# Prompt attention and three quarters of the output projection in one block of a hybrid decoder step

## The chip, the cores and the metric

The kernel runs on one core of a Trainium2 chip. A core has five engines with a queue of instructions each: PE (TensorE, the matrix engine), DVE (VectorE), ACT (ScalarE), POOL (GpSimd), and SP, which here only starts DMAs. Each engine runs its own queue strictly in the order written; engines wait for one another only at semaphores. The metric is the device time of one execution in microseconds (us), the median of several runs.

## The reference

One layer of a decoder, for a prompt (512 tokens and 16 learned "meta" tokens ahead of them) and 8 sample sequences of 4 tokens. All numbers are fp32. What matters here, for the prompt rows:

```python
# A: sparse attention. Per block of 128 queries: indexer scores over 16 small heads, top-128 keys, then 4 heads of attention
s = relu(einsum('bthd,bsd->bths', qi, ki)); sc = einsum('bths,bth->bts', s, wi)      # 16 heads, masked to the past
_, idx = lax.top_k(sc, topk)                                                          # topk = 128
logits = q . k[idx] + rel_bias[t5_bucket(dist)]; out = softmax(logits) @ v[idx]       # 4 heads x 128
# B (Mamba-2) and C (gated DeltaNet) give the other 1536 of 2048 columns, from the same normed input
mix = concatenate([o_a, o_b, o_c])          # 512 + 768 + 768 columns
x = x + mix @ w_out                         # 2048 x 2048
hm = rmsnorm(x, g_mlp); x = x + square(relu(hm @ w_up)) @ w_down    # 2048 x 8192 x 2048
```

Only the first 512 of the 2048 rows of `w_out` meet attention's output `o_a`; the other 1536 meet `o_b` and `o_c`, which are ready before attention starts.

## The kernel before

The program is a row of blocks with a barrier of all engines between them: an input projection (with sample attention beside it), convolutions and gates, the scans of B and C, `gate_and_norm`, `attention_inputs`, `attend_prompt`, and `output_and_mlp`.

**Projections.** An fp32 weight tile is split into a high and a low part, each good for the fast matmul form (fp32r), and three products are added: high by high, high weight by low activation, low weight by high activation. For the output projection a chunk is 128 output columns by 2048 rows (1 MB). SP loads it in two halves to `om_raw`; DVE masks it (`TENSOR_SCALAR`, `om_mask`), makes the high part (`CAST`), POOL subtracts for the low part (`TENSOR_TENSOR` to `om_ring`), and PE does 16 k tiles x 3 products x 2 halves of the 544 tokens = 96 matmuls into two PSUM banks. DVE then adds the banks to `om_x`. There are `NOUT` = 16 chunks, and the ring has two slots. The activations are split in the same way once, 16 tiles, at the start (L2846, L2850 on DVE, L2692 on POOL). After all 16 chunks, the second norm follows: squares (ACT) are summed by PE with a matrix of ones (L2740), DVE multiplies each of 16 tiles of x by the gain and splits it (L2870, L2846, L2850), and takes the reciprocal of the root (L2876); meanwhile the first MLP chunk runs as its tiles come. The MLP itself is a loop of 8 groups of 16 chunks, untouched by the change.

**Attention.** `attention_inputs` loads q, k, v and indexer rows, normalises q and k (DVE), turns them by PE transposes, and builds the relative bias (8 matmuls of a one-hot table, copied by DVE, written to DRAM and read back skewed into `toe`). `attend_prompt` goes over 5 query tiles, four of 128 rows and one of 16, with 128, 256, 384, 512 and 528 keys. For tile i >= 1: `choose(i)` adds up 16 indexer heads (PE score, ACT relu, DVE multiply and add, L1973), then 16 rounds of `MAX8` (L1979) and `MATCH_REPLACE8` (L1980) mark the 128 best keys; `soften(i)` does for each of 4 heads: PE scores, DVE adds mask and bias (L1994) and takes the maximum (L1996), ACT exponential, DVE reciprocal and scaling (L1998, L1999), PE transpose, ACT copy, PE product with v. One tile is finished before the next is begun on DVE. Score banks and the other buffers are double.

## Time and profile before

| what | value |
|---|---|
| median of 3 runs | 3852.7 us (3848.6 to 3852.73) |
| the profiled execution, its own time | 3852.63 us |
| its span in the profile | 3850.8 us |
| PE / DVE / POOL / ACT busy | 85% / 58% / 37% / 14% |
| `gate_and_norm` | 1650 to 1719 us |
| `attention_inputs` | 1719 to 1766.5 us |
| `attend_prompt` | 1766.5 to 2007.4 us |
| output projection with its start | 2007.4 to 2243.3 us |
| second norm beside the first MLP chunk | 2243.3 to 2277.2 us |
| the other 127 MLP chunks and the output | 2277.2 to 3850.8 us |

The first stage in the rows of stages below, 312 to 564 us, is the input projection beside the samples' selection.

Rows of the trace name the engine, the line of the kernel, the operation, the tile written and the tiles read. PEclk is the share of the full 2.4 GHz that TensorE was granted. Busy time of an engine that waits for another is no measure of the stage; what ends the waits is.

### The profile page before, as it was taken

Reading aid. Unit: us, or ns where it says so; the run is one execution under the profiler, and the core shown is the slowest. Engines: PE = TensorE matmul, PEld = TensorE weight load, DVE = VectorE, ACT = ScalarE, POOL = GpSimd, SP = SyncE. Lnnn points to the kernel's source line nnn. Section 1 sums busy time; section 2 is a strip of 40 time slices with the busy share of each in tenths; the row PEclk is TensorE's granted clock in tenths of the full one; section 3 lists DMA queues with packets and bytes.
Section 4 is the critical chain, followed back from the end, with each engine's and each line's share of the span. In section 5 each row is a group of like instructions: output and inputs, shape, how many; then the busy total and the mean of one; then the engine's idle time right before and its main releaser. Section 6 shows DMA issues by size and latency. Waiting matters only on the chain. (4 is left out here: it accounts for less than half of the span.)

```text
span 3850.8 us, 54189 instructions
## 1 busy us (share of the span) xinstructions
PE 3272.8 (85%) x22335; PEld 2978.1 (77%) x22335; DVE 2220.1 (58%) x3256; ACT 526.7 (14%) x1009; POOL 1409.3 (37%) x839
## 2 busy tenths in 40 slices
PE   7979997998944877715449989999999999999998
PEld 6927887997633777313129979999999999999998
DVE  6038985993176654446765465455555554646564
ACT  4132121121143111121121010000000000000000
POOL 4363332583332223110014344344444343444442
PEclk9999998999966987755669989999999999999999
DMA  5333332685420002142014213322323232223232
GB/s 175 88 94 100 90 89 82 188 273 155 142 86 24 1 1 66 28 159 85 0 60 140 81 55 90 86 88 85 92 82 91 80 88 89 88 86 91 78 93 96
DMA packets 412524, 352.99 MB, mean 92 GB/s; under 512 B 24106, under 2 KB 369290, under 8 KB 410901
## 3 DMA queue, kind: packets, MB, share of 16 engines
q1 hardware_dynamic: 383376, 285.58, 25.3%
q0 software_dynamic: 13440, 42.02, 3.4%
q10 hardware_dynamic: 15472, 21.90, 1.6%
q8 instruction: 190, 3.11, 0.3%
q14 instruction: 46, 0.38, 0.0%
HBM read 308.06 MB, written 42.61 MB: 91 GB/s over the span
## 5 line engine op out<-in xcount | busy, mean ns | idle before, releaser
L2686 POOL TENSOR_TENSOR om_ring<-om_raw,om_mask 128x1024 fp32r<-128x1024 f32 x288 | 741.0, 2573 | 1032.2 <-DVE om_ring L2789 1032.2
L2726 PE MATMUL om_ps<-om_h,om_ring 128*128 128x272 f32 x7680 | 986.8, 291 | 62.8 <-POOL om_h L2692 35.1
L2726 PEld LDWEIGHTS om_ps<-om_h,om_ring 128*128 128x128 f32 x7680 | 977.5, 191 | 70.1 <-issue 60.8
L2726 PE MATMUL om_ps<-om_hid,om_ring 128*128 128x272 f32 x6144 | 770.8, 288 | 0.0
L2726 PEld LDWEIGHTS om_ps<-om_hid,om_ring 128*128 128x128 f32 x6144 | 770.0, 188 | 0.0
L2789 DVE CAST om_ring<-om_mask 128x1024 fp32r<-128x1024 f32 x288 | 483.3, 1678 | 10.0
L320 POOL TENSOR_TENSOR w_ring<-w_raw,w_mask 128x1024 fp32r<-128x1024 f32 (+2 forms) x110 | 259.5, 2379 | 369.1 <-DVE w_mask L451 211.5
L371 PE MATMUL pm_ps<-h,w_ring 128*128 128x280 f32 x2688 | 364.2, 297 | 26.1 <-issue 11.5
L371 PEld LDWEIGHTS pm_ps<-h,w_ring 128*128 128x128 f32 x2688 | 355.5, 192 | 35.1 <-issue 28.0
L2797 DVE TENSOR_TENSOR om_x<-om_x,om_ps 128x272 f32<-128x272 f32 x288 | 112.8, 433 | 459.3 <-PE om_ps L2726 458.8
L389 PE MATMUL pq_ps<-w_ring,h 128*128 128x512 f32 (+2 forms) x1440 | 291.6, 365 | 7.6 <-POOL w_ring L320 7.5
L389 PEld LDWEIGHTS pq_ps<-w_ring,h 128*128 128x128 f32 x1440 | 249.0, 189 | 50.1 <-issue 8.3
L2914 ACT ACTIVATE om_relu<-om_relu 128x272 f32<-128x272 f32 x128 | 49.9, 432 | 1416.5 <-DVE om_relu L2818 1416.5
L2818 DVE SCALAR_TENSOR_TENSOR om_relu<-om_ps,om_rstd 128x272 f32<-128x272 f32 x128 | 50.4, 436 | 319.3 <-PE om_ps L2726 319.3
L2786 DVE TENSOR_SCALAR om_mask<-om_raw 128x1024 uint32<-128x1024 uint32 x288 | 209.2, 726 | 20.1 <-DMA om_raw<-in_w_out 17.6
L404 ACT ACTIVATE w_ring<-w_mask 128x1024 fp32r<-128x1024 f32 (+2 forms) x128 | 123.5, 1008 | 414.3 <-DVE w_mask L451 314.4
L451 DVE TENSOR_SCALAR w_mask<-w_raw 128x1024 uint32<-128x1024 uint32 (+2 forms) x128 | 85.7, 694 | 147.4 <-DMA w_raw<-in_w_in 146.5
L1950 POOL TENSOR_TENSOR ap_bm<-toe,ap_sc 128x128 f32<-128x128 f32 (+4 forms) x20 | 18.5, 945 | 295.3 <-DVE ap_sc L1982 194.6
L2406 POOL DMA_INDIRECT as_rows<-in_cache_v,as_offs x64 | 62.8, 982 | 106.1 <-PE as_o_bank L2571 93.5
L1881 PE MATMUL ap_t<-ident,ap_lg 128*128 128x128 f32 (+2 forms) x60 | 13.1, 334 | 102.3 <-DVE ap_lg L1999 102.3
L371 PEld LDWEIGHTS pi_ps<-h,w_ring 128*128 128x128 f32 x768 | 98.9, 188 | 0.1
L371 PE MATMUL pi_ps<-h,w_ring 128*128 128x280 f32 x768 | 98.9, 291 | 0.0
(475 smaller groups left out, 3438.0 us busy)
## 6 DMA issues: line engine op xcount, KB each, us to landing
om_raw<-in_w_up SPq DMA_DIRECT2D x128, 512.0 KB, 4.1
om_raw<-in_w_down SPq DMA_DIRECT2D x128, 512.0 KB, 3.6
w_raw<-in_w_in SPq DMA_DIRECT2D x112, 512.0 KB, 4.1
om_raw<-in_w_out SPq DMA_DIRECT2D x32, 512.0 KB, 4.1
as_qb<-q_rows SPq DMA_DIRECT2D x32, 256.0 KB, 5.1
projT<-pm_stage ACTq DMA_DIRECT2D x56, 140.0 KB, 2.1
conv_x<-projT SPq DMA_DIRECT2D x28, 280.0 KB, 2.8
xT_scratch<-ln_xT SPq DMA_DIRECT2D x1, 4480.0 KB, 16.0
```

The costliest lines, as they stand in the source:

```text
L320: eng.tensor_tensor(f32r(ring[:, n % 2, 1, half_of(q, n)]), raw[:, q, whole(q, n)], mask[:, q, whole(q, n)], ALU.subtract).then_inc(split[ ...
L371: ins = pe.matmul(ps[(b + y) % banks][:, 0:HALF], piece(a, k), f32r(h[:, x, k, two_halves(y)]), start=first, stop=last)
L389: ins = pe.matmul(ps[(b + m) % banks][:, 0:w], f32r(h[:, x, ld.k0 + k, tok]), piece(a, k), start=first, stop=last)
L404: act.activation(f32r(ring[:, n % 2, 0, half_of(q, n)]), mask[:, q, whole(q, n)], ACT.Copy).then_inc(hi_ready[q], 1)
L451: dve.tensor_scalar(bits(mask[:, q, whole(q, n)]), bits(raw[:, q, whole(q, n)]), HIGH, None, ALU.bitwise_and).then_inc(masked[q], 1)
L2406: pool.indirect_dma_start(self.rows[:, n % RING, :], None, table, bass.IndirectOffsetOnAxis(ap=self.offs[:, x, j:j + 1], axis=0)).then_inc ...
L2686: pool.tensor_tensor(f32r(ring[:, s, 1, half_of(q)]), raw[:, q, :], mask[:, q, :], ALU.subtract).then_inc(split[q], 1)
L2726: ins = pe.matmul(ps[bank][:, 0:HM], w, f32r(src[:, b, k, kept_half(half)]), start=first, stop=last)
L2786: dve.tensor_scalar(bits(mask[:, q, :]), bits(raw[:, q, :]), HIGH, None, ALU.bitwise_and).then_inc(masked_w[q], 1)
L2789: dve.tensor_copy(f32r(ring[:, s, 0, half_of(q)]), mask[:, q, :]).then_inc(hi_ready[q], 1)
L2797: dve.tensor_tensor(dst, dst, ps[b][:, 0:HM], ALU.add).then_inc(evac[b], 1)
L2818: dve.scalar_tensor_tensor(out=relu[:, 2 * (c % 2) + half, :], in0=ps[b][:, 0:HM], scalar=0.0, in1=rstd[:, kept_half(half)], op0=ALU.max, ...
```

## The change

1. `attention_inputs`, `attend_prompt` and 12 of the 16 k tiles of the output projection become one block, `attend_and_project`. The 12 k tiles are those of B and C. The projection there goes over 16 units of 128 output columns (72 matmuls and 768 KB of weights each, split in halves of 128x768), and adds to x tiles that are read from DRAM and written back (`ao_xin`). High parts of these weights are made by ACT, low parts by POOL; DVE masks and adds.
2. The order on every engine comes from `in_time`, which merges generators by due times written out by hand (`AS_FROM`, `AS_PER`, `UNIT` and others); the times only set the order.
3. Within attention DVE interleaves three query tiles: a round of selection on tile i, one head sum of tile i+1, and softmax steps of tile i-1. The last tile's 16 indexer heads are packed: 8 heads x 16 queries fill the 128 rows of one matmul, so that two relu tiles and a small matmul with `ao_selw` replace 16 steps.
4. The relative bias is built in `gate_and_norm` (PE, then ACT copies), ahead of its own work.
5. `output_and_mlp` keeps 4 k tiles: 4 chunks of 512 columns, 16 steps `t` of 24 matmuls, and gain and splitting of 12 of the 16 x tiles for the MLP are done inside that loop.

The core of the diff:

```diff
 def gate_and_norm(nc, dram, consts, sb):
         @block.scalar
         def _(act):
+            for x in range(8):
+                act.wait_ge(row, x + 1)
+                act.activation(rows_of_bias[:, x // 2, 384 * (x % 2):384 * (x % 2 + 1)], row_ps[x % 2][:, :], ACT.Copy
+                               ).then_inc(row_out, 1)
             for i in range(5):
...
+AS_FROM, AS_PER = (34.0, 46.0, 72.5, 111.0, 144.5, 178.0), (0.75, 1.65, 2.4, 2.1, 2.1, 3.0)
+FIRST_UNIT, UNIT = 10.0, 11.4
...
+def in_time(*streams):
+    due = [next(stream, None) for stream in streams]
+    while any(at is not None for at in due):
+        who = min((at, n) for n, at in enumerate(due) if at is not None)[1]
+        due[who] = next(streams[who], None)
...
+def attend_and_project(nc, dram, consts, sb):
...
+        def _(pe):
+            def weights():
+                for n in range(UNITS):
+                    for k in range(KB):
+                        yield unit_at(n) + UNIT / KB * k
+                        if k % (KB // PARTS) == 0:
+                            pe.wait_ge(hi_ready[k // (KB // PARTS)], n + 1)
+                            pe.wait_ge(split[k // (KB // PARTS)], n + 1)
...
+            in_time(inputs(), scores(), turns_of_weights(), values(), weights())
...
+        def _(dve):
...
+                for i in range(1, 5):
+                    for r in range(TOPP // 8):
+                        yield when(i, r)
+                        step(dve.max(best[0:n, r % 2, :], x))
+                        step(dve.match_replace(x, best[0:n, r % 2, :], x, TAKEN))
+                        if i < 3:
+                            add_head(i + 1, r)
...
+                        if i >= 2 and r % 4 == 1:
+                            yield logits_at(i - 1, r // 4)
+                            logits(i - 1, r // 4)
+                        if i >= 2 and r % 4 == 3:
+                            yield weights_at(i - 1, r // 4)
+                            normalise(i - 1, r // 4)
...
+            in_time(masks(), inputs(), attend(), sums())
...
 def output_and_mlp(nc, dram, sb):
-            for c in range(NOUT):
-                chunk(c, c % 2, h, KT, 2 * (c % 3), lambda b: c // 3 or None, tile_split(0) if c == 0 else None)
-                if c >= 2:
-                    add_squares(c - 2)
+            for t in range(KT):
+                n, m = t // NCH, t % NCH
+                for k in range(KA):
...
+                if t >= 2:
+                    add_squares(t - 2)
...
+            for t in range(KT):
+                if t % NCH == 0:
+                    before = t - 1
+                    highs(t // NCH + 1, (t // NCH + 1) % 2, (product[2 * (before % 3) + 1], before // 3 + 1) if t else None)
+                dve.wait_ge(x_in[t // 4], 16)
+                add_to_x((t,), 2 * (t % 3), lambda b: t // 3)
+                if 1 <= t <= KT - KA:
+                    gain(t - 1)
+            for k in range(KT - KA, KT):
+                gain(k)
```

PE in attention before, from the last head of tile 2 on: 15 of tile 3's indexer heads stand together (`ap_s` are the score banks, `ap_t` transposes, `ap_o` products with v).

```order
L1903 MATMUL ap_s<-kiT,qiT 128x512
L1881 MATMUL ap_t<-ident,ap_lg 128x128 x3
L1888 MATMUL ap_o<-ap_pT,v_tok 128x128 x3
L1903 MATMUL ap_s<-kiT,qiT 128x512 x15
L1906 MATMUL ap_s<-kT,qT 128x512 x2
```

PE now, in the middle of the selection on tile 1, where tile 2's heads are scored (`ao_w` are the projection's banks, six matmuls to a k tile):

```order
L1945 MATMUL ao_w<-ao_mh,ao_ring 128x272 x12
L1984 MATMUL ao_s<-ao_kiT,ao_qiT 128x384
L1945 MATMUL ao_w<-ao_mh,ao_ring 128x272 x12
L1984 MATMUL ao_s<-ao_kiT,ao_qiT 128x384
L1945 MATMUL ao_w<-ao_mh,ao_ring 128x272 x6
L1984 MATMUL ao_s<-ao_kiT,ao_qiT 128x384
```

Between two scores there now stand 6 to 12 projection matmuls, and the score of the next head waits behind them.

DVE now, at the same place (`ao_sc` are selection scores, `ao_xin` the x tiles of the projection):

```order
L2229 SCALAR_TENSOR_TENSOR ao_sc<-ao_relu,ao_wi,ao_sc 128x384
L2158 TENSOR_SCALAR ao_mask<-ao_raw 128x768 x2
L2281 MAX ao_best<-ao_sc 128x8
L2282 MATCH_REPLACE ao_sc<-ao_best,ao_sc 128x256
L2229 SCALAR_TENSOR_TENSOR ao_sc<-ao_relu,ao_wi,ao_sc 128x384
L2168 TENSOR_TENSOR ao_xin<-ao_xin,ao_w 128x272 x2
L2281 MAX ao_best<-ao_sc 128x8
```

Before, the 16 rounds of tile 1 stood alone, and the 16 head sums of tile 2 after tile 1's softmax; now each round has one head sum beside it, and once per unit two masks and two sums of the projection.

POOL in `output_and_mlp` before, up to the MLP (`om_hid` holds mix, `om_tile` the gained x tile):

```order
L2686 TENSOR_TENSOR om_ring<-om_raw,om_mask 128x1024 x2
L2692 TENSOR_TENSOR om_h<-om_hid,om_tile 128x544 x8
L2686 TENSOR_TENSOR om_ring<-om_raw,om_mask 128x1024 x32
L2692 TENSOR_TENSOR om_h<-om_tile 128x544 x8
L2686 TENSOR_TENSOR om_ring<-om_raw,om_mask 128x1024 x30
```

And now:

```order
L2987 TENSOR_TENSOR om_ring<-om_raw,om_mask 128x1024 x2
L2993 TENSOR_TENSOR om_h<-om_hid,om_tile 128x544 x2
L2987 TENSOR_TENSOR om_ring<-om_raw,om_mask 128x1024 x2
L2993 TENSOR_TENSOR om_h<-om_tile 128x544 x2
L2987 TENSOR_TENSOR om_ring<-om_raw,om_mask 128x1024 x2
L2993 TENSOR_TENSOR om_h<-om_tile 128x544 x2
```

The splitting of the gained tiles, eight in a row after the projection before, now stands in pairs between the four weight chunks.

## Rows read from the trace of the kernel before

**Rows 1.** Stages: us, busy PE, PEld, DVE, ACT, POOL, then PEclk, DMA share, GB/s.

```profile
312.00:564.00 252.00, 252.00 (x1167) 211.93 (x1166) 244.34 (x199) 49.21 (x62) 88.03 (x39) 1.00 0.32 94
...
1650.00:1719.00 69.00, 11.90 (x60) 9.76 (x60) 36.24 (x47) 20.64 (x34) 12.44 (x5) 0.55 0.31 115
1719.00:1766.50 47.50, 19.30 (x61) 11.88 (x61) 30.00 (x51) 5.61 (x6) 0.00 (x0) 0.57 0.76 246
1766.50:2007.40 240.90, 116.23 (x388) 62.00 (x388) 159.41 (x354) 53.25 (x129) 18.52 (x20) 0.61 0.01 5
2007.40:2243.30 235.90, 211.04 (x1601) 206.41 (x1601) 115.19 (x128) 23.23 (x36) 99.98 (x43) 0.96 0.39 119
2243.30:2277.20 33.90, 19.59 (x97) 16.83 (x97) 32.72 (x42) 9.87 (x15) 13.41 (x8) 0.77 0.00 0
```

**Rows 2.** Groups of DVE in `attend_prompt`, shapes apart; last columns: idle time before.

```profile
L1973 DVE SCALAR_TENSOR_TENSOR ap_sc<-ap_relu,wi,ap_sc 16x528 f32<-16x528 f32 x15 | 11.3, 756 | 2.4 <-ACT ap_relu L1924 1.9
L1979 DVE MAX8 ap_best<-ap_sc 128x8 f32<-128x512 f32 x16 | 11.1, 695 | 0.5
L1980 DVE MATCH_REPLACE8 ap_sc<-ap_best,ap_sc 128x512 f32<-128x512 f32 x16 | 10.8, 675 | 0.0
L1973 DVE SCALAR_TENSOR_TENSOR ap_sc<-ap_relu,wi,ap_sc 128x384 f32<-128x384 f32 x15 | 9.3, 619 | 8.1 <-ACT ap_relu L1924 7.8
...
L1979 DVE MAX8 ap_best<-ap_sc 128x8 f32<-128x256 f32 x16 | 6.8, 428 | 0.6
L1980 DVE MATCH_REPLACE8 ap_sc<-ap_best,ap_sc 128x256 f32<-128x256 f32 x16 | 6.5, 408 | 0.0
```

**Rows 3.** Timeline of PE at the end of the projection.

```profile
2224.84 12.39 PE L2726 MATMUL om_ps<-om_h,om_ring 128*128 128x272 f32 x96
2237.07 3.09 PE L2740 MATMUL om_ps<-om_tile,ones 128*128 128x272 f32 x12
```

**Rows 4.** Timeline of the start of `output_and_mlp`.

```profile
2007.39 1.02 SPq L2659 DMA_DIRECT2D om_raw<-in_w_out  x2
...
2017.96 2.94 DVE L2846 TENSOR_SCALAR om_tile<-om_hid 128x544 uint32<-128x544 uint32 x2
...
2022.24 6.75 PE L2726 MATMUL om_ps<-om_h,om_ring 128*128 128x272 f32 x36 [21.06 <-POOL om_h L2692]
...
2040.43 0.68 DVE L2786 TENSOR_SCALAR om_mask<-om_raw 128x1024 uint32<-128x1024 uint32 x1
...
2056.97 0.79 DVE L2797 TENSOR_TENSOR om_x<-om_x,om_ps 128x272 f32<-128x272 f32 x2 [2.98 <-PE om_ps L2726]
```

**Rows 5.** Timeline of `gate_and_norm`, attention's inputs, and attention's last instructions.

```profile
1658.04 1.48 ACT L1611 ACTIVATE gn_z<-gn_z 128x1536 f32<-128x1536 f32 x1 [6.37 <-DMA gn_z<-projN]
...
1736.23 1.21 DVE L1784 TENSOR_REDUCE ai_ss<-ai_sq 48x8 f32<-48x1024 f32 x1 [1.18 <-ACT ai_sq L1769]
...
1746.04 0.56 DVE L1787 COPY ai_rows<-ai_row 128x384 f32<-128x384 f32 x1 [0.72 <-PE ai_row L1816]
...
1979.45 0.16 DVE L1982 TENSOR_TENSOR ap_sc<-ap_sc,causal 16x16 f32<-16x16 f32 x1
...
2001.21 0.23 DVE L2001 COPY ap_outT<-ap_o 128x64 f32<-128x64 f32 x1 [3.56 <-PE ap_o L1888]
```

**Rows 6.** Timeline of DVE and POOL in the input projection, beside sample attention.

```profile
703.73 1.30 DVE L451 TENSOR_SCALAR w_mask<-w_raw 128x1024 uint32<-128x1024 uint32 x2
...
704.56 5.12 POOL L320 TENSOR_TENSOR w_ring<-w_raw,w_mask 128x1024 fp32r<-128x1024 f32 x2 [8.00 <-DVE w_mask L451]
704.94 2.49 DVE L2470 TENSOR_SCALAR as_near<-as_dist,as_drop 128x260 f32<-128x260 f32 x1
707.47 2.50 DVE L2472 TENSOR_TENSOR as_bias<-as_bias,as_near 128x260 f32<-128x260 f32 x1
710.00 0.35 DVE L2470 TENSOR_SCALAR as_near<-as_dist,as_drop 128x260 f32<-128x260 f32 x1
```

**Rows 7.** Selection for the samples: shortest, median and longest instruction, in ns.

```profile
L2321 DVE MAX8 sm_best<-sm_ssc x32: 2282/2291/2293, 312.4 to 558.6; 64x8 f32<-64x2052 f32 x32
```

More of the change, by code:

```diff
@@ L1679, in _ @@
         def _(pe):
+            pe.wait_ge(bias_in, 32)
+            for x in range(8):
+                if x >= 2:
+                    pe.wait_ge(row_out, x - 1)
+                pe.matmul(row_ps[x % 2][:, :], bc(rb[:, x // 2:x // 2 + 1], [32, P]),
+                          onehot[:, 384 * (x % 2):384 * (x % 2 + 1)], start=True, stop=True).then_inc(row, 1)
             for i in range(5):
@@ new lines, in attend_and_project @@
+        rows, keys = [P, P, P, P, TAILP], [P * (i + 1) for i in range(4)] + [TP]
+        blocks = lambda i: [(P * b, min(P, keys[i] - P * b)) for b in range(i + 1)]
+        relus = lambda i, h: HI * (i - 1) + h
+        half_of = lambda q: slice(UW // PARTS * q, UW // PARTS * (q + 1))
+        WIDE = TP // 2
+        wide = ((0, slice(0, WIDE)), (1, slice(WIDE, TP)))
+        order = [(when(0, h) - 2.5, "i", 1, h) for h in range(HI)]
+        order += [(when(i - 1, h) - 2.5, "i", i, h) for i in (2, 3) for h in range(HI)]
@@ new lines, in attend_and_project @@
+        order += [(when(3, 5), "w", 4, 0), (when(3, 6.5), "w", 4, 1), (when(3, 9), "s", 4, 0)]
+        order = sorted(order + [(logits_at(i, h) - 2.5, "h", i, h) for i in range(5) for h in range(HA)])
+        spans = {step[1:]: (1 if step[1] == "i" or step[1] == "h" and step[2] < 4 else 2) for step in order}
+        first_use, use = {}, 0
+        user = []
+        for step in order:
+            first_use[step[1:]] = use
+            user += [step[1:]] * spans[step[1:]]
+            use += spans[step[1:]]
@@ L1714, in attention_inputs, with lo_done, slot_free @@
+        bank = lambda step: s_ps[first_use[step] % 2]
+        both = lambda step: [(s_ps[(first_use[step] + x) % 2], part) for x, part in wide]
+        def lo_done(eng, k):
+            if k % 2:
+                eng.wait_ge(s["lo_odd"], k // 2 + 1)
+            else:
+                eng.wait_ge(s["lo_even"], k // 2 + 1)
+        def slot_free(eng, n):
+            if n >= 2:
+                eng.wait_ge(s["product"], 2 * (n - 1))
         block = ctx.enter_context(nc.Block())
@@ new lines, in positive @@
+            def positive():
+                for due, kind, i, h in order:
+                    step = (kind, i, h)
+                    if kind == "i":
+                        yield due + 1.2
+                        act.wait_ge(s["score"], nth[step] + 1)
+                        if relus(i, h) >= 2:
+                            act.wait_ge(s["acc"], relus(i, h) - 1)
+                        act.activation(relu[:, h % 2, 0:keys[i]], bank(step)[:, 0:keys[i]], ACT.Relu).then_inc(s["relu_out"], 1)
+                    if kind == "w":
+                        yield due + 1.5
+                        act.wait_ge(s["score"], nth[step] + 1)
+                        act.wait_ge(s["acc"], relus(4, 0) - 1 + h)
+                        for ps, part in both(step):
+                            act.activation(relu[:, h, part], ps[:, 0:WIDE], ACT.Relu).then_inc(s["relu_out"], 1)
@@ new lines, in exps, with turned_out @@
+            def exps():
+                for c in range(5 * HA):
+                    i, h = c // HA, c % HA
+                    n, one = rows[i], lg[0:rows[i], c % 2, 0:keys[i]]
+                    yield logits_at(i, h) + 1.2
+                    act.wait_ge(s["lg_ready"], c + 1)
+                    act.activation(one, one, ACT.Exp, bias=mx[0:n, c % 2:c % 2 + 1], accum_out=den[0:n, c % 2:c % 2 + 1]
+                                   ).then_inc(s["exp_ready"], 1)
+            def turned_out():
+                for c in range(5 * HA):
+                    i, h = c // HA, c % HA
+                    n = rows[i]
+                    yield weights_at(i, h) + 2.0
+                    act.wait_ge(s["p_turned"], c + 1)
+                    if c >= 2:
+                        act.wait_ge(s["pv"], c - 1)
+                    last = act.activation(pT[:, c % 2, 0:n * min(i + 1, 4)], t_ps[:, 0:n * min(i + 1, 4)], ACT.Copy)
+                    if i == 4:
+                        last = act.activation(pT[0:n, c % 2, 4 * n:5 * n], t_ps[0:n, 4 * n:5 * n], ACT.Copy)
+                    last.then_inc(s["pT_out"], 1)
@@ L2891, in tile_high @@
                 act.wait_ge(masked, n + 1)
[L2892 to L2894 removed]
+                act.activation(f32r(h[:, 0, place(n), :]), tile[:, 2 + n % 2, :], ACT.Copy).then_inc(h_hi, 1)
+            for k in range(KA):
                 tile_high(k)
```

842 lines of the change are left out of this document (504 added, 338 removed).

## The prediction, written before the changed kernel ran

> **What bounds the kernel now.** I read the table of stages first [rows 1], since the change touches only 1650 to 2277 us. Attention's two blocks take 288.4 us (1719.0 to 2007.4), and no engine is full in them: in `attend_prompt` DVE works 159.4 of 240.9 us, PE 116.2 at a granted clock of 0.61. The reader is to see a chain that passes from engine to engine. The projection with its start is the reverse, 235.9 us with PE busy for 211.0 at a clock of 0.96: there PE is the bound. The 33.9 us after it are DVE's (32.7 busy), which splits 16 tiles while PE waits. From 1719.0 to 2277.2, where the second MLP chunk starts, it is 558.2 us. After that the work is unchanged. The sum is made against the profiled execution, 3852.63 us, which lies 0.07 us under the median, so one serves for the other.
>
> **PE's work in the new block.** A full chunk of 96 matmuls takes 12.39 us [rows 3], 0.129 us each, and a k tile of six 0.774 us. 16 units of 72 are 1152 x 0.129 = 149 us. Attention's matmuls are fp32: in [rows 3] 12 instructions of 272 columns take 3.09 us at the high clock, 0.26 each, and each call is two of them, so a call costs about 1.9 ns a column. Columns of scores: 16 heads x (256 + 384 + 512), 4 x 264 for the packed tile and as many for its sums, 4 x (128 + 256 + 384 + 512 + 528) for the logits; with v 40 x 128 and 20 x 16. That is 33,200 columns, 64 us, and 60 transposes that I put at 0.15 us (one instruction of 128 columns by the same rate is 0.12) make 73. PE together: 222 us at 2.4 GHz, besides the inputs' transposes.
>
> **DVE's work in the new block.** `attend_prompt` has 159.4 us [rows 1]. Gone are the last tile's 16 head sums, 16 x 0.76 = 12 [rows 2], against 1.6 for what replaces them. The inputs had 30.0 [rows 1], of which eight bias copies of 0.56 = 4.5 go [rows 5]. The projection adds 32 masks (0.69 us for 1024 columns [rows 4], so by columns 0.55 for 768) 17.6, 16 pairs of sums of 0.79 [rows 4] 12.6, and the splitting of 12 tiles 9. Sum 213 us, with gaps of 0.03 us between instructions some 220. So neither PE nor DVE can finish the block much under 225 us, against 288.4 for attention alone before; but both are nearly full at once, and each waits for the other in order.
>
> **What POOL takes from DVE.** In [rows 6] two weight subtractions of POOL run 704.56 to 709.68, and DVE instructions that take 0.35 us alone take 2.49 and 2.50 beside them: DVE gets one instruction in between two POOL ones, and loses 4.2 of 5.1 us. Not every instruction suffers. `MAX8` on 2052 keys took 2282 to 2293 ns in all 32 cases [rows 7], though POOL worked 88 of those 252 us [rows 1]. So selection runs on, and head sums, masks, scalings and normalisation (two SBUF inputs, or the fast copy form) are held. The Trainium skill, GPSIMD Engine Reference, Specifications, says that GpSimd shares its SBUF interfaces with VectorE, with contention for instructions in a two-port mode or with two SBUF inputs. By that rule the trace agrees, and a plan that adds only busy times is too short. Here POOL has 2 x 1.8 us a unit (0.75 of the 2.4 at 1024 columns). Beside selection rounds of 1.0 to 1.4 us a held head sum waits some 0.7 us per subtraction, 1.4 a unit, in seven units; the four units before it lose about 3 each; the rest 0.5: 25 us in all. If all of it were held it would be 0.82 x 58 = 47, if none, nothing.
>
> **The block, stage by stage.** *Start.* Before, the first tile was masked 10.6 us after the first DMA, and 16 tiles took to 2040.4, 22.5 us [rows 4]; 12 take 17, so 27 us. Then five reductions in turn with ACT's squares, 1.21 + 1.18 = 2.4 us apart [rows 5], 12, with ACT's two high parts (1.6) in between 14. Then normalising and turning, which took 1746.6 to 1766.5 before, 20 us [rows 5], now with two units' masks and POOL's holds, and PE's turns behind 2 to 3 k tiles each: 27. Attention proper starts at 68 us. PE has done only 2 of 16 units by then. *Five phases*, by the greater of PE and DVE and 5 to 10% for waiting on each other: the heads of tile 1 (PE 21, DVE 18) 23; selection 1 with heads 2 (16 x (0.99 + 0.65) = 26 on DVE [rows 2], masks, sums and holds 8; PE 33) 36; selection 2 with heads 3 and the softmax of tile 1 (PE 52, DVE 50) 55; selection 3 with softmax 2 (PE 40, DVE 40) 43; selection 4 with softmax 3 (PE 38, DVE 41) 43. *Tail.* The last four softmax heads, which took 1979.6 to 2001.4 before, 22 us [rows 5], now with 1.3 units of matmuls between them: 27. *End*: from the last copy to the next block's first DMA 6 us, as before. Sum 68 + 227 + 6 = 301 us. Attention before took 288.4: the new block costs about 13 us more than attention did, and hides 12 of 16 k tiles.
>
> **The rest of the projection.** The start to the first matmul stays 14.9 us [rows 4], and the first step waits for its 4 tiles, 5. A step `t` is 24 x 0.129 + 4 x 0.26 = 4.1 us of PE. DVE and POOL, which hold each other, need per 4 steps 8.3 us of held DVE work and 7.8 of POOL, 4.0 a step: so near to PE that I take 4.8. 15 steps are 72, and this part is 92 us. Then the first MLP chunk, 12.4 us, has 12 of its 16 tiles ready; DVE has four left, 7 us, waits for the root, takes the reciprocal and masks the second chunk: 20 us to the second chunk instead of the 40.1 from 2237.1 to 2277.2. Together 112 against 269.8 (2007.4 to 2277.2).
>
> **The bias in `gate_and_norm`.** The eight products and copies came 0.56 + 0.72 = 1.28 us apart [rows 5]. Now ACT does them ahead of the silu that starts at 1658.04 [rows 5], its first work there. With their table in about 4 us after the stage starts, the last copy ends near 1664.6, 6.6 us later; the five silus behind it no longer wait for their loads and win some of it back: +4.5 us. Floor 0 (if the table is there sooner), ceiling 6.6.
>
> **Sum.** 558.2 - (4.5 + 301 + 112) = 140.7, and 3852.6 - 141 = 3712, say **3710 us**. About 0.2% (8 us) is what a measurement can tell from no change.
>
> **Rivals.**
> *The block at its floor.* Interleaving works so well that only DVE's 220 us, the 5 us before its first data, 13 us of the tail and the end count, and few holds: 255 us. For it: selection is always there to fill waits. Against it: the start, where DVE has no selection to do and PE stands still. 3710 - 46 = 3664 us. Chance 0.22.
> *Coupling.* PE's scores stand behind up to 12 projection matmuls (1.55 us), score banks are two deep, and the order by hand leaves out masks and holds, so that each late event delays both engines. Phases at 1.25 times the greater engine instead of 1.06 are 268 for 227, with a start of 72: the block 345 us. For it: before, a DVE busy for 159 needed 241. 3755 us. Chance 0.23.
> *The clock, and slower than before.* Where PE was busy for 116 of 241 us it was granted 0.61, where it was busy for 211 of 236, 0.96 [rows 1]. If the block's mix of short matmuls and waits kept PE at its low level of 1.2 GHz, its 203 us after the start (222 less two units) would be 406, the block 68 + 406 + 6 = 480, and the kernel 3710 + 179 = 3889. The break-even block is 558.2 - 4.5 - 112 = 442 us, so it decides from a mean clock below 203 / (442 - 74) = 0.55. Against it: at the low clock PE would be full, and full stages here have 0.96 to 1.00. Chance 0.02. [...]
> *The projection is not hidden*, because a weight transfer, x tiles or the saving of keys block SP's one queue ahead of something needed: a unit needs 0.77 MB and 0.56 MB of x traffic per 14 us, 95 GB/s, where 246 GB/s have been moved [rows 1]. Only if that cost 8 us in each of 16 units would it eat the gain; 3840 us or so, no change. Chance 0.01.
> My forecast has the remaining 0.52, with its own range of 3685 to 3735.
>
> **How the numbers follow.** The range reaches into the two neighbours, to 3660 and 3757, and leaves out some 0.2. Faster 0.97, same 0.01 and slower 0.02 are the sums of these cases.
>
> **What would show it.** In the changed profile: attention proper (the first `ao_sc` head sum) starting 60 to 75 us after the block's first DMA, 290 to 315 us from that DMA to the next block's; PE over 85% busy from there to the tail at a clock over 0.9; DVE busy for about 245 with holds in it (head sums of 384 columns averaging 0.9 us rather than 0.62, `MAX8` unchanged at 0.43 to 0.70); steps of 4.2 to 5.5 us in `output_and_mlp`, and about 20 us from its last step to the second MLP chunk; the first silu near 1664. The prediction is wrong if phases run at 1.25 of the busier engine, or the start is under 50 us, or the clock sags in selection.

## The result and the profile after

The changed kernel takes 3720.53 us (median of 4 runs, 3716.98 to 3724.62) against 3851.98 for the kernel before on the same chip: a ratio of 0.9661, 95% interval 0.9644 to 0.9677. It is faster, by 131 us. The forecast was 3710 us with a range of 3660 to 3757. In its profiled execution the span is 3715.1 us, 135.7 less than before. The forecast's sum had 140.7.

The first view is the table of stages of the changed kernel, with the columns of [rows 1]. The rows are, in order: `gate_and_norm`; the block's start up to the first head sum; the heads of tile 1; selection up to its last `MAX8`; the tail to the next block's first DMA; the start of `output_and_mlp`; its steps; and from the last product of the steps to the second MLP chunk.

```profile
1650.90:1727.40 76.50, 21.87 (x76) 14.06 (x76) 38.10 (x47) 24.24 (x42) 12.44 (x5) 0.57 0.34 125
1727.40:1803.70 76.30, 34.62 (x192) 31.23 (x193) 51.20 (x71) 18.23 (x26) 21.05 (x14) 0.67 0.70 222
1803.70:1843.30 39.60, 37.59 (x136) 25.63 (x136) 17.79 (x38) 13.15 (x33) 8.79 (x7) 0.66 0.12 36
1843.30:2009.60 166.30, 161.80 (x1023) 130.98 (x1022) 150.35 (x328) 48.04 (x92) 55.07 (x35) 1.00 0.32 97
2009.60:2041.80 32.20, 25.85 (x192) 21.79 (x190) 13.55 (x33) 5.02 (x17) 5.20 (x4) 0.92 0.14 52
2041.80:2063.20 21.40, 8.14 (x45) 8.17 (x46) 11.85 (x10) 2.52 (x4) 8.27 (x4) 0.56 0.98 354
2063.20:2122.00 58.80, 56.05 (x392) 53.79 (x391) 54.82 (x76) 17.79 (x27) 29.89 (x14) 0.97 0.24 74
2122.00:2141.00 19.00, 15.56 (x113) 14.61 (x112) 15.88 (x17) 5.44 (x8) 5.80 (x3) 1.00 0.01 1
```

The block takes 314.3 us (1727.4 to 2041.8), and the rest of the projection up to the second MLP chunk 99. Before, the same places were 288.4 and 269.8 [rows 1]. In selection PE is busy for 161.8 of 166.3 us at a granted clock of 1.00, with DVE close behind at 150.4. The heads of tile 1 stand out: PE is busy there too, 37.6 of 39.6 us, but at 0.66. Three places cost more than forecast, and the next views show them.

The timeline of ACT in `gate_and_norm` shows the copies of the bias rows, 1.28 us apart with PE as their releaser, and the silus behind them:

```profile
1655.72 0.49 ACT L1621 ACTIVATE gn_mix<-gn_row 128x384 f32<-128x384 f32 x1 [50.38 <-PE gn_row L1701]
...
1664.68 0.49 ACT L1621 ACTIVATE gn_mix<-gn_row 128x384 f32<-128x384 f32 x1 [0.79 <-PE gn_row L1701]
1665.19 1.28 ACT L1626 ACT_TABLE_LOAD   x1
1666.48 2.86 ACT L1626 ACTIVATE gn_z<-gn_z 128x1536 f32<-128x1536 f32 x2
```

The first silu starts at 1666.48, where it started at 1658.04 before [rows 5]. Of the 8.4 us, 1.3 are a table load that now stands behind the copies instead of in idle time at the stage's start.

The timeline of DVE shows the block's start. The number in brackets is the idle time before the instruction, with what ended it:

```profile
1753.40 0.22 DVE L2187 TENSOR_SCALAR ao_qn<-ao_qn 128x128 f32<-128x128 f32 x1
1763.12 0.56 DVE L2158 TENSOR_SCALAR ao_mask<-ao_raw 128x768 uint32<-128x768 uint32 x1 [9.50 <-issue]
1764.37 1.60 DVE L2158 TENSOR_SCALAR ao_mask<-ao_raw 128x768 uint32<-128x768 uint32 x1 [0.69 <-DMA ao_raw<-in_w_out]
1765.89 1.21 DVE L2191 TENSOR_REDUCE ao_ss<-ao_sq 128x8 f32<-128x1024 f32 x1
```

DVE stands for 9.5 us before unit 1's weights. The view names no releaser for it, so SP's own timeline has to show it: the small loads for the indexer run from 1738.4, and unit 1's weights come behind them.

```profile
1738.43 0.92 SPq L1878 DMA_DIRECT2D ao_ki<-projN  x2
...
1749.36 3.72 SPq L1881 DMA_DIRECT2D ao_wq<-projN  x8
1753.12 0.43 SPq L1883 DMA_DIRECT2D ao_qiT<-projT  x1
1753.59 3.50 SPq L1860 DMA_DIRECT2D ao_raw<-in_w_out  x2
```

At the start of the heads of tile 1, the timelines of DVE, POOL and PE, and then a table of short stretches with the columns of [rows 1]:

```profile
1803.74 1.91 DVE L2227 TENSOR_SCALAR ao_sc<-ao_relu,ao_wi 128x256 f32<-128x256 f32 x1
1805.68 1.91 DVE L2229 SCALAR_TENSOR_TENSOR ao_sc<-ao_relu,ao_wi,ao_sc 128x256 f32<-128x256 f32 x1
...
1809.65 0.48 DVE L2229 SCALAR_TENSOR_TENSOR ao_sc<-ao_relu,ao_wi,ao_sc 128x256 f32<-128x256 f32 x1
...
1803.62 3.69 POOL L2126 TENSOR_TENSOR ao_ring<-ao_raw,ao_mask 128x768 fp32r<-128x768 f32 x2 [0.22 <-PE ao_w L1945]
...
1805.26 0.70 PE L1984 MATMUL ao_s<-ao_kiT,ao_qiT 64*128 64x256 f32 x2
1807.97 1.22 PE L1984 MATMUL ao_s<-ao_kiT,ao_qiT 64*128 64x256 f32 x2 [2.01 <-DVE ao_big L2244]
```

```profile
1800.00:1806.00 6.00, 5.67 (x36) 3.99 (x34) 5.79 (x10) 2.18 (x5) 3.06 (x3) 1.00 0.19 63
1806.00:1808.00 2.00, 0.03 (x1) 0.03 (x1) 1.93 (x3) 0.38 (x2) 1.90 (x2) 1.00 0.45 134
1808.00:1834.00 26.00, 26.00 (x76) 17.89 (x78) 7.83 (x21) 6.17 (x16) 0.92 (x2) 0.50 0.14 42
...
1836.00:1844.00 8.00, 8.00 (x45) 5.67 (x44) 6.07 (x15) 3.77 (x9) 3.67 (x2) 1.00 0.12 36
```

The rows show a chain of four links. POOL works on two weight subtractions for 3.7 us. DVE's head sums take 1.91 us beside them, and 0.48 once POOL is done. PE, whose score bank DVE empties, stands for 2.0 us. The granted clock, 1.00 in the 6 us before, goes to 0.50, the 1.2 GHz level, and PE works for 26 us at half speed before it comes back. From then on `PEclk` is 1.00 until selection ends.

Last, PE in the steps of `output_and_mlp`, and DVE behind the last one:

```profile
2114.30 1.08 PE L3041 MATMUL om_ps<-om_tile,ones 128*128 128x272 f32 x4
2115.01 3.36 PE L3061 MATMUL om_ps<-om_h,om_ring 128*128 128x272 f32 x24
2118.21 1.08 PE L3041 MATMUL om_ps<-om_tile,ones 128*128 128x272 f32 x4
...
2063.23 0.69 DVE L3102 TENSOR_SCALAR om_mask<-om_raw 128x1024 uint32<-128x1024 uint32 x1 [5.23 <-DMA om_raw<-in_w_out]
...
2136.34 0.69 DVE L3102 TENSOR_SCALAR om_mask<-om_raw 128x1024 uint32<-128x1024 uint32 x1 [0.35 <-DVE om_rstd L3196]
```

A step is 3.91 to 3.93 us, in which PE's matmuls follow one another without a wait. Ahead of the steps DVE waits 5.23 us for the second chunk of weights.

### The profile page after: what moved, and what is told of

Same layout as the page of the kernel before. It is cut to its first block and busy times, and to the rows that moved or that the text cites. A ratio compares the mean times of both kernels' runs of the same rounds, so it can differ in the third digit from the quotient of the medians.

```text
span 3715.1 us, 54246 instructions
## 1 busy us (share of the span) xinstructions
PE 3254.6 (88%) x22287; PEld 2969.2 (80%) x22287; DVE 2200.4 (59%) x3253; ACT 548.6 (15%) x1038; POOL 1410.8 (38%) x847
## 5 line engine op out<-in xcount | busy, mean ns | idle before, releaser
L2987 POOL TENSOR_TENSOR om_ring<-om_raw,om_mask 128x1024 fp32r<-128x1024 f32 x264 | 681.2, 2580 | 934.0 <-DVE om_ring L3105 934.0
L3027 PE MATMUL om_ps<-om_h,om_ring 128*128 128x272 f32 x6144 | 778.8, 289 | 21.8 <-issue 18.3
L3027 PEld LDWEIGHTS om_ps<-om_h,om_ring 128*128 128x128 f32 x6144 | 776.1, 190 | 24.3 <-issue 24.1
L3105 DVE CAST om_ring<-om_mask 128x1024 fp32r<-128x1024 f32 x264 | 457.2, 1732 | 9.2
L1945 PE MATMUL ao_w<-ao_mh,ao_ring 128*128 128x272 f32 x1152 | 184.5, 313 | 32.2 <-ACT ao_mh L2043 32.2
L1945 PEld LDWEIGHTS ao_w<-ao_mh,ao_ring 128*128 128x128 f32 x1152 | 161.9, 202 | 62.6 <-issue 49.7
L3102 DVE TENSOR_SCALAR om_mask<-om_raw 128x1024 uint32<-128x1024 uint32 x264 | 182.3, 690 | 16.9 <-DMA om_raw<-in_w_out 15.2
L2126 POOL TENSOR_TENSOR ao_ring<-ao_raw,ao_mask 128x768 fp32r<-128x768 f32 x32 | 61.9, 1953 | 200.7 <-DVE ao_mask L2158 140.6
```

The source lines that it names most:

```text
L1945: ins = pe.matmul(w_ps[2 * (n % 2) + half][:, 0:HM], w, f32r(mh[:, b, k, kept_half(half)]), start=first, stop=last)
L2126: pool.tensor_tensor(f32r(ring[:, n % 2, 1, half_of(q)]), raw[:, q, :], mask[:, q, :], ALU.subtract).then_inc(split[q], 1)
L2987: pool.tensor_tensor(f32r(ring[:, s, 1, half_of(q)]), raw[:, q, :], mask[:, q, :], ALU.subtract).then_inc(split[q], 1)
L3027: ins = pe.matmul(ps[bank][:, 0:HM], w, f32r(src[:, b, k, kept_half(half)]), start=first, stop=last)
L3102: dve.tensor_scalar(bits(mask[:, q, :]), bits(raw[:, q, :]), HIGH, None, ALU.bitwise_and).then_inc(masked_w[q], 1)
L3105: dve.tensor_copy(f32r(ring[:, s, 0, half_of(q)]), mask[:, q, :]).then_inc(hi_ready[q], 1)
```

## Experiments

All times of stretches below are differences of starts in the traces: the gate stage runs from `gate_and_norm`'s norm weights to the block's first DMA, then start, heads of tile 1, selection and tail as above, and "to the root" from `output_and_mlp`'s first DMA to its reciprocal.

| kernel | ratio to before (95%) | gate | start | tile 1 | selection | tail | to the root |
|---|---|---|---|---|---|---|---|
| changed | 0.9661 (0.9644 to 0.9677) | 75.2 | 76.3 | 39.6 | 166.3 | 32.2 | 90.7 |
| e1 unit 1 first | 0.9639 (0.9625 to 0.9652) | 75.3 | 66.7 | 39.3 | 166.3 | 32.1 | 90.5 |
| e2 copies on DVE | 0.9652 (0.9639 to 0.9665) | 70.7 | 77.7 | 39.6 | 166.3 | 32.1 | 91.0 |
| e3 fill PE | 0.9627 (0.9614 to 0.9640) | 75.7 | 76.2 | 29.9 | 166.3 | 32.1 | 90.7 |
| e4 gain after | 0.9720 (0.9707 to 0.9733) | 75.3 | 75.9 | 39.4 | 166.4 | 32.1 | 110.2 |
| e5 narrow lows | 0.9631 (0.9614 to 0.9647) | 75.1 | 73.3 | 23.7 | 167.1 | 33.1 | 88.9 |
| e6 no units | 0.9490 (0.9475 to 0.9506) | 75.3 | 59.7 | 24.4 | 132.7 | 29.9 | 91.6 |
| e7 changed again | 0.9660 (0.9645 to 0.9676) | 76.0 | 76.4 | 39.2 | 166.3 | 32.2 | 90.5 |
| e8 three edits | 0.9593 (0.9578 to 0.9609) | 70.8 | 67.2 | 30.3 | 166.3 | 32.2 | 90.9 |
| e9 unit 3 later | 0.9618 (0.9602 to 0.9633) | 70.9 | 67.0 | 35.5 | 166.3 | 32.2 | 89.2 |
| e10 chunk 1 first | 0.9650 (0.9634 to 0.9665) | 75.4 | 76.3 | 39.5 | 166.3 | 32.1 | 86.2 |
| e11 more PE work | 0.9676 (0.9663 to 0.9690) | 75.3 | 77.4 | 37.9 | 174.5 | 33.0 | 90.5 |
| e12 four edits | 0.9578 (0.9564 to 0.9592) | 70.6 | 66.4 | 30.3 | 166.2 | 32.2 | 86.1 |

The ratios' intervals are some 6 us wide to each side, so the small effects are read in the stretches, which mostly repeat within 1 us in kernels that don't touch them, and within 2 in all. What follows the root took 1578.9 to 1584.2 us in these traces, with the same work, which is one reason why a ratio and the sum of the stretches differ by a few us. A hundredth of a ratio is 38.5 us.

**e1, unit 1's weights first.** The small loads move into a function of their own that SP runs behind unit 1's weights.

```diff
+                    if n == 1:
+                        more_inputs()    # ki, wi, wq and qiT loads, out of first_inputs()
```

> Edit: SP issues the weights of the second unit right behind the q and k rows, ahead of the 24 small loads (indexer keys, head weights, queries) that they stood behind. Theory A (SP's queue is what the start waits for): in the changed kernel DVE stands 9.5 us for these weights with nothing else to do; it no longer stands there, the first head sum comes 67 instead of 76 us after the block's first DMA, and the time is 3720.5 - 9 = 3711 us. Rival B (the transfers are the limit, since the DMA engines are 77 to 103% busy in that stretch): what is moved back is late instead, and the time stays within 3 us of 3720. Rival C: the start is shorter but phase 0 only starts at a lower clock and gives it back: first head sum at 67, block still about 314.

Measured: the first head sum comes 66.7 instead of 76.3 us after the block's first DMA, and nothing else moves. The granted clock in the heads of tile 1 stays 0.65, so nothing is given back. Theory A holds. The DMA engines were busy for 79% of this start, and could take the weights earlier: SP's order was the wait, not the transfers.

**e2, the bias copies on DVE.**

```diff
-                act.activation(rows_of_bias[:, x // 2, 384 * (x % 2):384 * (x % 2 + 1)], row_ps[x % 2][:, :], ACT.Copy
+                dve.tensor_copy(rows_of_bias[:, x // 2, 384 * (x % 2):384 * (x % 2 + 1)], row_ps[x % 2][:, :]
```

> Edit: in gate_and_norm the eight copies of the bias rows are made by DVE, which has nothing to do then, instead of by ACT ahead of its silus. Theory A (the copies and the table load behind them delay ACT's silus): first silu back at 1658, the block after this one begins 6 to 8 us earlier, 3713 us. Rival B: the copies end near 1665 as before, since PE makes a row in 1.28 us, and DVE's gating products then start at 1665 instead of 1659.5; the squares wait for them, and only 2 to 3 us come back: 3718 us.

Measured: the first silu starts 7 us earlier, but the stage ends only 4.5 us earlier. DVE's timeline shows why:

```profile
1679.28 0.56 DVE L1660 COPY gn_mix<-gn_row 128x384 f32<-128x384 f32 x1 [0.72 <-PE gn_row L1701]
1679.76 7.65 DVE L1665 TENSOR_TENSOR y_ssd<-y_ssd,gn_z 128x768 f32<-128x768 f32 x5
```

The gating products come right behind the last copy, 7.3 us after the first silu (1672.47). So rival B's mechanism holds: the rows themselves, 1.28 us of PE each, are what the stage now waits for, and the engine that copies them only decides who waits. The stage gave somewhat more than B's 2 to 3 us. The start behind it took 1.4 us more in this run (77.7 for 76.3), so the first head sum came 3.1 us earlier; in e8, e9 and e12, which hold the same edit, the start did not grow.

**e3, PE filled.** Behind each of the first five score steps PE makes two products into a bank that is free.

```diff
                     last.then_inc(s["score"], 1)
+                    if nth[step] < 5:
+                        pe.wait_ge(s["out"], 10)
+                        for x in range(2):
+                            pe.matmul(o_bank[:, 0:256], sb["ident"][:, :], kT[:, 0, 0:256], start=True, stop=True)
```

> Edit: behind each of the first five score steps PE makes two products of 256 columns that nobody reads (about 5 us of extra PE work), into a bank that is free then. Nothing is left out. Theory A (PE's idle 2.0 us at 1806, in which DVE is held by POOL, is what lets the granted clock fall from 1.00 to 0.50 for 26 us): the clock stays up, the heads of tile 1 take 26 instead of 39.6 us, and the time is 3708 us. Rival B (the clock falls for the idle stretches before, which the edit does not touch): 39.6 plus up to 5 us, 3720 to 3726 us.

Measured, the heads of tile 1, with the columns of [rows 1]:

```profile
1815.50:1845.40 29.90, 29.90 (x158) 21.25 (x156) 16.62 (x38) 12.97 (x33) 8.73 (x7) 1.00 0.16 48
```

The clock stays at 1.00, and the phase takes 29.9 instead of 39.6 us although PE has some 5 us more to do. Adding work that nobody needs makes the kernel 13 us faster by its ratio and 9.7 by its trace. The phase is 4 us longer than the 26 expected. DVE and POOL at its start:

```profile
1815.45 0.34 DVE L2231 TENSOR_SCALAR ao_sc<-ao_relu,ao_wi 128x256 f32<-128x256 f32 x1
1817.29 1.04 DVE L2233 SCALAR_TENSOR_TENSOR ao_sc<-ao_relu,ao_wi,ao_sc 128x256 f32<-128x256 f32 x1 [1.50 <-ACT ao_relu L2083]
...
1816.23 3.79 POOL L2130 TENSOR_TENSOR ao_ring<-ao_raw,ao_mask 128x768 fp32r<-128x768 f32 x2 [1.11 <-PE ao_w L1945]
```

So the edit did more than fill. The first products stand ahead of the projection matmuls that POOL waits for, its subtractions begin 0.8 us behind the first head sum instead of 0.1 ahead of it, and the first two sums take 0.34 and 1.04 us where they took 1.91 each. Theory A holds in its last link: where PE does not stand, the clock stays up. How much of it is the filling and how much the later subtractions, this run does not separate.

**e4, one part undone: gains behind the steps.**

```diff
-                if 1 <= t <= KT - KA:
-                    gain(t - 1)
-            for k in range(KT - KA, KT):
+            for k in range(KT):
                 gain(k)
```

> Edit: one part undone. In output_and_mlp the gains and splits of the 16 tiles come behind the last step of the projection again, instead of 12 of them between the steps. Theory A (as I forecast: DVE's splitting beside PE's steps is free): the stretch from the last step to the second MLP chunk grows from about 19 to 40 us, the steps stay 4.1 to 4.3 us; 3741 us. Rival B (DVE and POOL set the steps' length): the steps fall to 3.9 us and give 4 to 8 us back; 3733 us.

Measured: 19.5 us more to the root, 23 by the ratio. PE's steps are 3.92 us as before. Theory A holds: in the changed kernel, splitting 12 tiles between the steps is free, and worth the 20 us forecast for it.

**e5, POOL's subtractions made narrow.**

```diff
+                        w = UW // PARTS if n < 2 else 8
+                        pool.tensor_tensor(f32r(low[:, 0:w]), raw[:, q, 0:w], mask[:, q, 0:w], ALU.subtract
```

> Edit: POOL's subtractions for the weights of units 2 to 15 cover 8 columns instead of 768, so their low parts are left out (what stands in the ring from units 0 and 1 is used instead); every wait and matmul stays. It prices what POOL's 28 subtractions of 1.8 us take from DVE. Theory A (as forecast, 25 us of DVE's time is held, but in the two phases where PE is 100% busy this costs nothing): 8 to 12 us less, 3710 us. Rival B (the block is DVE's, every held us counts): 25 us less, 3696 us. Rival C (holds are hidden by PE altogether): no change, 3720 us. In all cases head sums of 512 columns fall from 0.985 towards 0.75 us.

Measured: the three stretches from the block's first DMA to the last `MAX8`, and DVE's head sums:

```profile
1737.00:1810.30 73.30, 34.60 (x192) 31.48 (x193) 48.04 (x71) 18.22 (x26) 17.77 (x14) 0.66 0.72 231
1810.30:1834.00 23.70, 23.70 (x127) 16.57 (x126) 13.35 (x38) 11.47 (x31) 2.12 (x7) 1.00 0.22 62
1834.00:2001.10 167.10, 163.28 (x1032) 132.15 (x1031) 143.06 (x329) 49.24 (x95) 17.85 (x34) 1.00 0.33 97
```

```profile
L2231 DVE SCALAR_TENSOR_TENSOR ao_sc<-ao_relu,ao_wi,ao_sc 128x512 f32<-128x512 f32 x15 | 11.3, 755 | 8.2 <-ACT ao_relu L2079 7.9
L2231 DVE SCALAR_TENSOR_TENSOR ao_sc<-ao_relu,ao_wi,ao_sc 128x384 f32<-128x384 f32 x15 | 9.3, 618 | 5.5 <-ACT ao_relu L2079 5.3
```

In the changed kernel these groups have means of 985 and 701 ns:

```profile
L2229 DVE SCALAR_TENSOR_TENSOR ao_sc<-ao_relu,ao_wi,ao_sc 128x512 f32<-128x512 f32 x15 | 14.8, 985 | 4.1 <-ACT ao_relu L2079 3.8
L2229 DVE SCALAR_TENSOR_TENSOR ao_sc<-ao_relu,ao_wi,ao_sc 128x384 f32<-128x384 f32 x15 | 10.5, 701 | 3.3 <-ACT ao_relu L2079 2.9
```

The time fell by 12 us by the ratio, in theory A's range, yet for another reason than A's; the stretches in the table add up to 19. The three rows above lose 3.2, 4.4 and 7.3 us of DVE's busy time, 14.9 in all where I had 25. (Units 0 and 1 and the mix tiles keep their subtractions, so 14.9 is the price of 28 of 32, and a lower bound of all holds.) In selection that is worth nothing (167.1 against 166.3): what DVE no longer loses there it waits for ACT and PE, as the 8.2 us of idle time beside 4.1 show. In the start it is worth 3 us. In the heads of tile 1 it is worth 15.9 us, far more than the 4.4 us held, since PE never stands there, and the clock stays at 1.00.

**e6, the block without its projection.** `UNITS = 1`: 15 of the 16 units, with their weights, masks, sums and x tiles, are left out.

```diff
-UNITS = D // P
+UNITS = 1
```

> Edit: of the 16 units of the projection in the block only the first is done; the matmuls, weights, masks, sums and x tiles of the other 15 are left out. It shows what the interleaved attention takes by itself, and so what the projection costs inside the block. Theory A (both engines are nearly full with it, so the units cost what PE needs beyond attention's own): attention alone takes 215 to 240 us, the projection costs 75 to 100 us in the block where it cost 150 us and its splitting before; the interleaving is worth as much as the hiding. 3630 to 3645 us. Rival B (interleaving brings nothing by itself and the projection rides in the waits): block 285 to 300 us, 3690 to 3705 us.

Measured: the block takes 246.7 us, a little above A's bounds and far below B's, and the kernel 3660 us, 15 above A's. Against the 288.4 of attention before, the new form of attention is worth 41.7 us, even with the first unit and its 12 mix tiles aboard. That is not the interleaving alone: the last tile's packed heads and the bias copies, which moved out, are in it. The copies alone kept DVE from its last reduction to the reciprocal before, 9 us (1737.4 to 1746.5, [rows 5]). No run separates the three. The other 15 units cost 67.4 us (314.1 in e7 less 246.7), a little under A's 75 to 100: 4.5 each, where their 72 matmuls are 9.3 us at full clock. By stretches they cost 16.7 us in the start, 14.8 in the heads of tile 1, where the clock falls, 33.6 in selection and 2.3 in the tail.

```profile
1824.70:1957.40 132.70, 93.77 (x199) 42.04 (x199) 122.64 (x282) 31.37 (x70) 11.92 (x12) 0.58 0.00 0
```

Without the units selection belongs to DVE, 122.6 of 132.7 us, and PE does attention's matmuls at a clock of 0.58. With them the clock is 1.00, and of PE's 161.8 us in selection 121.5 are the projection's, which leaves some 40 for the attention matmuls that take 93.8 here. That makes room for part of the units.

**e7, the changed kernel again.**

> The changed kernel itself, unedited, so that the small effects of this group are read against it on the same chip: 0.966 of the kernel before.

Measured: 0.9660, and the same stretches within 0.8 us.

**e8, three edits together,** those of e1, e2 and e3.

> Edit: unit 1's weights first, the bias copies on DVE, and PE's ten products that nobody reads, together. Measured alone in their traces they shortened the stretch they touch by 9.9, 3 and 10 us. Theory A (three separate causes): 21 to 23 us less than the changed kernel of the same call. Rival B (they share a cause, the low granted clock at the start of phase 0, which each of them may lift by chance): 10 to 14 us less.

Measured: 3691.82 us beside 3718.03 for e7, 26 us less, and in the stretches 5.2, 9.2 and 8.9 us less: 23.3. The sum of the three alone, 9.6, 4.5 and 9.7, is 23.8. Theory A holds, three separate causes; the medians give a little more than its 21 to 23.

**e9, the hold moved instead of filled.** The edits of e1 and e2, and unit 3's masks, high and low parts 4 us of due time later on DVE, ACT and POOL.

```diff
-                    yield unit_at(n - 1) + 0.5 if n else 0.5
+                    yield unit_at(n - 1) + 0.5 + (4.0 if n == 3 else 0.0) if n else 0.5
```

> Edit: unit 1's weights first and the copies on DVE as before, no filling; instead the masks, high and low parts of unit 3 come 4 units of due time later, behind the first heads of tile 1, so that POOL does not hold DVE's first head sum (1.91 us instead of 0.48). Theory A (the held DVE leaves PE idle, and that idle stretch brings the granted clock down): the clock stays near 1.00 through phase 0, which takes 24 to 27 us instead of 37; as fast as the filled kernel or 2 us faster. Rival B (the hold only moves and stalls PE later in the phase): the clock falls all the same, only at another place, and it is 10 us slower than the filled kernel.

Measured, DVE, PE, and four stretches:

```profile
1800.61 2.03 DVE L2233 SCALAR_TENSOR_TENSOR ao_sc<-ao_relu,ao_wi,ao_sc 128x256 f32<-128x256 f32 x1
...
1803.01 1.22 PE L1988 MATMUL ao_s<-ao_kiT,ao_qiT 64*128 64x256 f32 x2 [2.28 <-DVE ao_big L2248]
```

```profile
1797.00:1802.00 5.00, 3.74 (x21) 2.55 (x20) 3.18 (x6) 3.87 (x7) 1.63 (x1) 1.00 0.00 0
1802.00:1807.00 5.00, 3.99 (x10) 2.46 (x11) 3.27 (x7) 1.42 (x5) 2.90 (x3) 0.56 0.44 116
1807.00:1817.00 10.00, 10.00 (x33) 7.05 (x32) 2.60 (x7) 1.43 (x4) 0.00 (x0) 0.50 0.25 78
1817.00:1827.00 10.00, 10.00 (x48) 7.01 (x49) 5.64 (x13) 4.72 (x13) 3.54 (x2) 0.86 0.02 6
```

The hold moved 9 us later, PE stood for 2.28 us there, and the clock fell at that place. Rival B holds: the phase takes 35.5 us, against 30.3 in e8 with its 5 us of filling aboard, and the kernel is 9 us slower than e8 by the medians. It is the strongest evidence for the chain, since the fall moved with the hold. With e5, where POOL's subtractions are narrow, PE does not stand and the clock stays at 1.00, it shows both ends of the chain.

**e10, chunk 1 ahead of the x tiles.**

```diff
+            load(1, lambda q: out[q][:, :, WIDE:2 * WIDE])
             for q in range(4):
                 sp.dma_start(x[:, 4 * q:4 * q + 4, :], x_t[:, 4 * q:4 * q + 4, META:]).then_inc(x_in[q], 16)
-            for c in range(1, NCH):
+            for c in range(2, NCH):
```

> Edit: in output_and_mlp SP issues the second chunk of weights ahead of the 16 x tiles, as the kernel before did. Theory A (SP's order makes DVE wait 5.2 us for this chunk, and with it all steps): 3 to 5 us less than the changed kernel. Rival B (the DMA engines are 98% busy there, so the x tiles come later by what the chunk comes earlier, and the first additions wait instead): no change, within 1 us.

Measured: 4.5 us less to the root (86.2), 3.7 by the medians. Theory A holds, although the DMA engines were 98% busy in that stretch: what came later, the x tiles, was needed later.

**e11, more work for PE in selection.**

```diff
+                        if k == 0 and 5 <= n < 14:
+                            for x in range(12):
+                                pe.matmul(w_ps[2 * (n % 2) + x % 2][:, 0:HM], f32r(ring[:, n % 2, 0, 0:P]),
+                                          f32r(mh[:, 0, 0, kept_half(x % 2)]), start=True, stop=True)
```

> Edit: nine of the units, 5 to 13, all in the selection phases, make their first twelve matmuls with extra ones ahead that are overwritten: 12 more of 272 columns each, 0.129 us at the granted clock of 1.00, 1.55 us a unit, 13.9 us in all. Nothing is left out. Theory A (selection with its units is PE's: PE is busy for 161.8 of 166.3 us there): 12 to 14 us more than the changed kernel, about 3731. Rival B (DVE, busy for 150 of 166, and the waits between the two set the length): 0 to 5 us more, since PE's few gaps and DVE's chain absorb it.

Measured:

```profile
1854.60:2029.10 174.50, 173.92 (x1127) 143.98 (x1126) 148.88 (x329) 47.92 (x93) 54.89 (x35) 1.00 0.31 93
```

Selection takes 8.2 us more, between the two theories; the kernel takes 5.8 more by the ratio. PE's busy time grew by 12.1 us to 173.9 of 174.5: the first 4 us went into the gaps that PE had, all in the phases of tiles 3 and 4, and everything beyond lengthened the stretch one for one. PE is the bound of selection, with 4.5 us of gaps in 166.3.

**e12, four edits.** Those of e8 and e10.

> Edit: the three edits of the fastest kernel so far (unit 1's weights first, the bias copies on DVE, ten products that nobody reads) and the second chunk of weights ahead of the x tiles. Theory A (the fourth is independent of them): 4 us less than with three, 0.9583 of the kernel before, 3688 us. Rival B (the fourth overlaps with what the others gave): no less than with three, 0.9593.

Measured: 0.9578 against 0.9593 for e8, with the root 4.8 us earlier than in e8. Against the kernel before it is 4.2% faster, against the changed kernel 0.9%.

## Why the prediction was right, and where it was right by luck

The direction, the place and the mechanism held, and the sum missed the saving by 5 us of 140.7. Term by term the errors were larger, and they cancelled.

**The block: 301 forecast, 314.3 measured.**
- *Start, 68 against 76.3.* Masks of the mix tiles took 26 of the 27 us forecast, the reductions with unit 1's masks 16.5 (1763.1 to 1779.6) for 14, and normalising and turning 24 of 27. What failed is the step that let unit 1's weights cost nothing: I priced the masks and holds beside them, not that DVE's order puts their wait ahead of the reductions, and not the 24 small DMAs that SP has to issue first. From the last mix tile to unit 1's mask it is 9.7 us (1753.4 to 1763.1). The forecast's rival "not hidden" named SP's queue, but only for the steady units. e1 measures the term by taking it away: 9.6 us.
- *Heads of tile 1, 23 against 39.6.* The step that failed is PE's 21 us, taken at full clock from the rate of [rows 3]. I treated the clock as a matter of the whole block and found it safe, since full stages have 0.96 to 1.00. It fell in one phase of a nearly full block, because one hold left PE idle for 2.0 us. e5 and e9 show this, and e3 the last link. The Trainium skill, TensorE: Matmul & The Clock Gate, What's actually happening, has the throttled clock as the default that activity lifts. The trace agrees in part: the clock fell once PE had stood and rose again under matmuls, but before it rose, 26 us of uninterrupted matmuls passed at the low level.
- *Selection, 177 forecast to its last mask, 168.9 measured* (1843.3 to 2012.2). The phases were 36.7, 51.8 and 80.4 us for 36, 55 and 86. "The greater of PE and DVE and 5 to 10%" was too careful: in the first two phases PE was busy for every us. e11 confirms PE as the bound; without the units it is DVE (e6).
- *Holds, 25 against 14.9 us of DVE,* and in selection they cost no time (e5). The rule behind them (some instructions are held, `MAX8` not) held: 128x512 head sums went from 755 to 985 ns, and `MAX8` on 512 keys took 689 ns, where it took 695 before [rows 2]. Its size was too large: head sums of 384 columns averaged 701 ns, not the 0.9 us that the forecast gave as a sign, and DVE was busy for 232.9 us in the block's four stretches, not 245.
- *Tail 24 for 27, end 5.7 for 6.*

**The rest of the projection: 112 forecast, 99 measured.** The steps were 3.92 us, not 4.8. I let DVE's and POOL's held work set the step at 4.0 and added to it. It is PE's 3.92 (I had 4.1), and held work beside a full PE costs nothing, the same mistake as in selection. 15 steps of 0.88 too much are the 13 us. The 20 us behind the last step were 19, and e4 shows that they would be 20 longer without the interleaved gains. The start took 21.4 us for 20: the first matmul came after 13.3 us instead of 14.9, and the 5.2 us wait for chunk 1 was missing from the sum. e10 gives 4.5 of it back.

**The bias: 4.5 forecast, with a ceiling of 6.6, measured 7.8** (76.5 us for 68.7 from the stage's first DMA). The ceiling was wrong: I left out the silu table's load behind the copies (1.28 us), and believed that the five silus would win time back. They did run without a wait between them (five in 7.0 us), but DVE's products behind them gained nothing from it: its second reduction came 8.4 us later than before, as the first silu did. POOL's five products stand beside DVE's five for 12.4 us in both kernels, and from the first to the last DVE's took 10.9 us in both, where one alone takes 0.96: it seems that they were held, and I had left this hold out. No run shows it. In e2, 4.5 of it comes back.

So +13.3, -13 and +3.3 stand against each other. That they cancelled was luck. The likeliest case's own range, 3685 to 3735, would have held any one of them. The "coupling" rival did not come true: the phases and the tail took 232.4 us, not its 268 (227 forecast), though in the heads of tile 1 a late event did delay both engines, through the clock. The "floor" rival's 255 us was not reached either: with POOL's subtractions narrow the block takes 297.2 us, and without the projection 246.7.

The 136 us saved in the trace add up as follows: the new form of attention (interleaved, packed, its bias built elsewhere), with one unit aboard, gives 41.7 (e6); the rest of the projection falls by 170.8 (269.8 - 99), of which the gains between the steps are some 20 (e4); against it stand 67.6 for 15 units in the block (314.3 - 246.7), 7.8 for the bias and 0.6 of an offset that was there before it: 136.5.

## What to carry to other kernels

When two engines are both nearly full, ask first which one is at 100%. Here extra work on it cost one for one once its 4.5 us of gaps in 166 were full (e11), and 7.3 us taken off the other, busy for 150 of 166, gave nothing (e5). How much the other could have taken on was not tested. Look at each place where a phase begins: one late event there that left TensorE idle for 2 us cost 10 us or more through its clock, and giving TensorE work that nobody needs was worth more than moving the delay (30.3 us against 35.5, e8 and e9). And where one engine issues all transfers in program order, walk through that order at the start of a block and put first what the busiest engine will wait for first, even when the DMA engines look full.
